# Expert passes of a mixture-of-experts step: token rows fetched by row number from device memory instead of by a product on TensorE

## The reference, cut to what matters

```python
logits = x.astype(f32) @ w_router.astype(f32) + b_router.astype(f32)
top_val, top_idx = lax.top_k(logits, TOP_K)
top_w = jax.nn.softmax(top_val, axis=-1)
gates = jnp.einsum('blk,blke->ble', top_w, jax.nn.one_hot(top_idx, N_EXPERTS, dtype=f32))
out = jnp.zeros(x.shape, f32)
for e in range(N_EXPERTS):
    out = out + gates[..., e:e + 1] * swiglu(x, wg[e], wu[e], wd[e]).astype(f32)
```

## Time and profile before

| what | value |
| --- | --- |
| median of 3 runs | 1713.34 us (1710.79 to 1714.33) |
| the profiled execution | 1714.72 us |
| its span in the trace | 1713.0 us |
| granted TensorE clock, mean over the span | 0.978 |
| PE busy | 1641.1 us (96%) |
| DVE busy | 1357.7 us (79%) |
| ACT busy | 1001.2 us (58%) |
| POOL busy | 59.1 us (3%) |

### The profile page before, as it was taken

The page is one execution under the profiler, slowest core; times in us unless marked ns, Lnnn a source line. Parts: engine busy times, 40 slices in busy tenths (PEclk is TensorE's granted clock), DMA queues, the critical chain, the costliest instruction groups (busy, mean ns, idle before and its releaser), DMA issues.

```text
span 1713.0 us, 25673 instructions
## 1 busy us (share of the span) xinstructions
PE 1641.1 (96%) x9611; PEld 1398.7 (82%) x9611; DVE 1357.7 (79%) x1480; ACT 1001.2 (58%) x923; POOL 59.1 (3%) x84
## 2 busy tenths in 40 slices
PE   7999999999999998999999999999999999999993
PEld 3878889998899797888888888888888888888883
DVE  5836656767676676988988988998988988989985
ACT  1222544443445236777777777777777777777771
POOL 2002000000000202000000000000000000000002
PEclk9999999999999999999999999999999999999997
DMA  6444245555354326999999999998998998998980
GB/s 160 128 135 123 91 143 165 180 160 173 108 158 155 82 74 220 321 376 336 348 376 326 354 373 329 347 376 329 353 371 314 371 368 313 375 372 309 370 331 25
DMA packets 209696, 441.84 MB, mean 258 GB/s; under 512 B 22896, under 2 KB 26912, under 8 KB 209614
## 3 DMA queue, kind: packets, MB, share of 16 engines
q1 hardware_dynamic: 205518, 435.18, 72.4%
q0 software_dynamic: 2048, 4.29, 1.4%
q10 hardware_dynamic: 2064, 1.45, 0.4%
HBM read 437.06 MB, written 1.93 MB: 256 GB/s over the span
## 4 chain that ended last, share of the span: by engine, by line
PE 80%; DVE 10%; issue 4%; ACT 2%; DMA 2%; SPq 1%; POOL 1%; DVEq 0%; ACTq 0%; POOLq 0%
PE bank L1642 77%; PE bank L1645 3%; DVE w_lo L991 2%; DVE piece_lo L991 2%; DVE ssm L991 2%; ACT piece_hi L735 1%; ACT y_hi L925 1%; DMA r_all<-in_b_glu_dram 1%; DMA piece<-in_w_proj_a_dram 1%; DVE r_all L991 0%; DVE wide L1405 0%; DVE ssm L1439 0%; DMA piece<-in_w_ffn_gate_dram 0%; DVE y_lo L1529 0%; DVE scr L991 0%
## 5 line engine op out<-in xcount | busy, mean ns | idle before, releaser
L991 DVE TENSOR_TENSOR w_lo<-weights,w_hi 128x2048 fp32r<-128x2048 f32 x336 | 765.1, 2289 | 98.6 <-ACT w_hi L934 94.7
L934 ACT ACTIVATE w_hi<-weights 128x2048 fp32r<-128x2048 f32 x336 | 644.4, 1920 | 191.3 <-PE bank L1642 191.2
L1642 PE MATMUL bank<-w_hi,xg_hi 128*128 128x512 f32 x896 | 357.4, 399 | 6.5 <-DVE xg_lo L991 5.0
L1642 PE MATMUL bank<-w_hi,xg_lo 128*128 128x512 f32 x896 | 350.6, 391 | 0.0
L1642 PE MATMUL bank<-w_lo,xg_hi 128*128 128x512 f32 x896 | 349.8, 390 | 0.0
L991 DVE TENSOR_TENSOR piece_lo<-piece,piece_hi 128x1024 fp32r<-128x1024 f32 x126 | 150.8, 1221 | 107.5 <-ACT piece_hi L735 104.3
L735 ACT ACTIVATE piece_hi<-piece 128x1024 fp32r<-128x1024 f32 x126 | 129.5, 1054 | 146.5 <-PE bank L1642 111.7
L1642 PEld LDWEIGHTS bank<-w_hi,xg_hi 128*128 128x128 f32 x896 | 168.6, 188 | 45.7 <-issue 6.9
L1642 PEld LDWEIGHTS bank<-w_hi,xg_lo 128*128 128x128 f32 x896 | 168.5, 188 | 36.9
L1642 PEld LDWEIGHTS bank<-w_lo,xg_hi 128*128 128x128 f32 x896 | 168.9, 189 | 32.9
L1642 PE MATMUL bank<-w_hi,hidT_hi 128*128 128x512 f32 x448 | 175.0, 391 | 0.0
(11 more groups left out here) (315 smaller groups left out, 2156.2 us busy)
## 6 DMA issues: line engine op xcount, KB each, us to landing
weights<-in_w_moe_gate_dram SPq DMA_DIRECT2D x112, 1024.0 KB, 7.3
weights<-in_w_moe_up_dram SPq DMA_DIRECT2D x112, 1024.0 KB, 7.3
weights<-in_w_moe_down_dram SPq DMA_DIRECT2D x112, 1024.0 KB, 6.8
piece<-in_w_in_dram SPq DMA_DIRECT2D x48, 512.0 KB, 3.8
piece<-in_w_ffn_gate_dram SPq DMA_DIRECT2D x22, 512.0 KB, 4.6
piece<-in_w_ffn_up_dram SPq DMA_DIRECT2D x22, 512.0 KB, 4.4
piece<-in_w_ffn_down_dram SPq DMA_DIRECT2D x22, 512.0 KB, 3.9
piece<-in_w_out_dram SPq DMA_DIRECT2D x16, 512.0 KB, 4.4
```

Source lines behind the costliest of these rows:

```text
L934: act.activation(w_hi[s % PAIRS][:, :], ring_slot[:, :], ACT.Copy).then_inc(w_hi_ready, 1)
L991: return dve.tensor_tensor(out, a, b, op)
L1642: signals(pe.matmul(out, lhsT, rhs, start=start, stop=stop, skip_group_check=True), signal)
```

## The change

The three tiles of token rows are no longer kept in SBUF in two parts. ACT copies them only into `acc`, and POOL writes them from there to device memory (`token_rows`, 264 rows of 1024, three DMAs). TensorE multiplies `pick` by a two-column tensor `token_no` that holds each token's number (three matmuls of two columns, `which_rows`), DVE converts the result to int32 (`which_i`), and POOL fetches the 128 rows that these numbers name into `xrow` by an indirect DMA (`gather`). In a pass this is done at chunk f = 4 (`NFC - 3`), for the next pass. The 12 matmuls of `rows_picked` and the two copies into `xrow` are gone, in the loop and ahead of it. The transposes of `xrow` stay where they were. POOL now runs the loop too. The loads of `ln2_g` and `ln2_b` stand behind POOL's loop.

```diff
+    if _f == NFC - 3:
+        PASS_TILES += [(("which",), "d", 6)]
+PASS_TILES += [(("hT", NFC - 1), "d", 6 + (NFC - 1) % 2)]
-PASS_TILES += [(("hT", NFC - 1), "d", 6 + (NFC - 1) % 2), (("picked", 0), "a", 2), (("picked", 1), "d", 3)]
...
+            for h, (at, m) in enumerate(TILES):
+                pool.wait_ge(emptied["a"], tiles.count["a"] - 6 + 2 * h + 2)
+                pool.dma_start(token_rows_dram[at:at + m, :], acc[0:m, h, :]).then_inc(rows_kept, 16)
+            pool.wait_ge(rows_kept, 16 * 3)
+            def gather():
+                pool.indirect_dma_start(out=xrow[:, :], out_offset=None, in_=token_rows_dram[:, :],
+                                        in_offset=bass.IndirectOffsetOnAxis(ap=which_i, axis=0)).then_inc(row_gathered, 16)
+            def turn():
+                pool.tensor_tensor(gather_turn, ones[:, 0:1], ones[:, 0:1], ALU.mult).then_inc(gather_turns, 1)
+            turn()
+            pool.wait_ge(which_ready, 1)
+            gather()
+            with all_passes(pool) as i:
+                wait_pass_emptied(pool, ("which",), i)
+                pool.wait_ge(xg_hi_ready, i * 2 + 2)
+                pool.wait_ge(gather_turns, i + 1)
+                turn()
+                gather()
...
-            act.wait_ge(router_zero, 1)
             for i in range(6):
-                p, h, at, ps = token_rows(i)
-                act.activation(xtok_hi[p, h, at], ps, ACT.Copy).then_inc(xtok_hi_ready, 1)
-                if i >= 3:
-                    act.activation(acc[p, h, at], ps, ACT.Copy).then_inc(emptied["a"], 1)
-            act.wait_ge(xtok_lo_ready, 3)
-            for i in range(3):
                 p, h, at, ps = token_rows(i)
                 act.activation(acc[p, h, at], ps, ACT.Copy).then_inc(emptied["a"], 1)
...
                 slots(pick, sel_of, 0, pick_ready)
+                dve.wait_ge(first_which, 1)
+                dve.tensor_copy(which_i, bank[0][:, 0:1]).then_inc(which_ready, 1)
...
+                        if f == NFC - 3:
+                            dve.wait_ge(row_gathered, i * 16 + 16)
+                            dve.tensor_copy(which_i, pass_tile_in(dve, ("which",), i)[:, 0:1]).then_inc(emptied["d"], 1)
                 hidden_lo(NFC - 1)
-                dve.tensor_copy(xrow[:, 512:D], pass_tile_in(dve, ("picked", 1), i)[:, :]).then_inc(emptied["d"], 1)
...
+            def which_rows(ps, signal):
+                for h in range(3):
+                    mm(ps[:, 0:2], pick[:, h, :], token_no[:, h, :], h == 0, h == 2, signal if h == 2 else None)
+            which_rows(bank[0], first_which)
             mm(bank[pass_bank[("ye", 0)]][:, :], spread[:, 0:P], y_hi[:, 0:512], True, True, filled)
+            fill(bank[pass_bank[("ye", 1)]], 12)
+            pe.wait_ge(row_gathered, 16)
...
+                        if f == NFC - 3:
+                            pe.wait_ge(pick_ready, i + 2)
+                            which_rows(claim_in_pass(("which",), i), filled)
                         down(f - 1)
                 hidden_transposed(NFC - 1)
-                pe.wait_ge(pick_ready, i + 2)
-                rows_picked(i)
                 down(NFC - 1)
```

More of the change, by code:

```diff
@@ L293, in trunk_kernel @@
             ssm = shared.enter_context(nc.sbuf_tensor("ssm", [P, SSM], F32))
-        xtok_hi = sb("xtok_hi", [P, 3, D], F32R)
-        xtok_lo = sb("xtok_lo", [P, 3, D], F32R)
         y_hi = sb("y_hi", [P, D], F32R)
@@ L299, in trunk_kernel @@
         spread = sb("spread", [P, 3 * P], F32R)
-        ROUTER = 2 * 3 * D + 2 * D + 2 * 3 * P
+        ROUTER = 2 * D + 2 * 3 * P
         sb("rest_of_ssm", [P, SSM - ROUTER])
@@ L440, in trunk_kernel @@
         ones = ssm[:, 19008:19008 + P]
-        assert 8960 == ROUTER
+        token_no = nc.alloc_sbuf_tensor_at("token_no", [P, 3, 2], F32R, offset=ssm_at + 4 * 19136)
+        token_i = ssm[:, 19144:19147].bitcast(I32)
+        which_i = ssm[:, 19152:19153].bitcast(I32)
+        gather_turn = ssm[:, 19160:19161]
+        token_rows_dram = nc.dram_tensor("token_rows", [T, D], F32, kind="Internal").ap()
         prm = r_all[0:96, 0:P]
@@ L483, in trunk_kernel @@
         xg_hi_ready, hidT_hi_ready = map(sem, ("xg_hi_ready", "hidT_hi_ready"))
-        first_picked, first_row_by_act, first_row_by_dve = map(
-            sem, ("first_rows_picked", "first_row_by_act", "first_row_by_dve"))
+        first_which, which_ready, rows_kept, row_gathered, gather_turns = map(
+            sem, ("first_rows_found", "rows_found", "token_rows_stored", "token_rows_gathered", "gather_turns"))
         router_zero, gslot_zero = map(sem, ("router_tiles_zero", "gslot_zero"))
-        xtok_hi_ready, xtok_lo_ready, xtok_lo_of_pool, y_hi_ready, spread_ready = map(
-            sem, ("xtok_hi_ready", "xtok_lo_ready", "xtok_lo_of_pool", "y_hi_ready", "spread_ready"))
+        y_hi_ready, spread_ready = map(sem, ("y_hi_ready", "spread_ready"))
         fvar_ready, fstd_ready, fscale_ready, y_out, y_out_step, y_stored = map(
@@ L693, in _ @@
             pool.memset(y_lo[:, :].bitcast(F32), 0.0).then_inc(router_zero, 1)
+            step(pool.iota(token_i, pattern=[[P, 3]], base=0, channel_multiplier=1))
+            pool.memset(token_no[:, :, :].bitcast(F32), 0.0).then_inc(router_zero, 1)
+            pool.wait_ge(router_zero, 7)
+            pool.tensor_copy(token_no[:, :, 0:1], token_i.unsqueeze(2)).then_inc(router_zero, 1)
             pool.wait_ge(router_zero, 8)
[L695 to L700, removed]
+            for h, (at, m) in enumerate(TILES):
[16 more added lines that the diff above has]
+                gather()
             for i, name in enumerate(("ln2_g", "ln2_b")):
@@ L963, in one_pass @@
                 hidden_hi(NFC - 1)
[L964 to L968, removed]
             act.wait_ge(npass_ready, 1)
@@ L1435, in slots @@
                 if ready is pick_ready:
-                    dve.wait_ge(router_zero, 3)
+                    dve.wait_ge(router_zero, 1)
                 for h, (_, m) in enumerate(TILES):
@@ L1481, in routing @@
                     dve.tensor_copy(sel_of[:, :, at], SEL)
[L1482 to L1487, removed]
                 ps = tile_in(dve, ("pos",))
@@ L1614, in _ @@
             routing()
-            dve.wait_ge(first_picked, 2)
-            dve.tensor_copy(xrow[:, 512:D], bank[1][:, :]).then_inc(first_row_by_dve, 1)
             dve.wait_ge(npass_ready, 1)
@@ L1952, in _ @@
             pe.wait_ge(sel_ready, 1)
-            pe.wait_ge(router_zero, 5)
+            pe.wait_ge(router_zero, 3)
             ps = claim(("pos",))
@@ L1966, in _ @@
             pe.wait_ge(router_zero, 8)
-            pe.wait_ge(xtok_lo_ready, 3)
-            pe.wait_ge(xtok_lo_of_pool, 3)
             pe.wait_ge(pick_ready, 1)
+            def which_rows(ps, signal):
+                for h in range(3):
+                    mm(ps[:, 0:2], pick[:, h, :], token_no[:, h, :], h == 0, h == 2, signal if h == 2 else None)
+            which_rows(bank[0], first_which)
             mm(bank[pass_bank[("ye", 0)]][:, :], spread[:, 0:P], y_hi[:, 0:512], True, True, filled)
+            fill(bank[pass_bank[("ye", 1)]], 12)
+            pe.wait_ge(row_gathered, 16)
             for n in range(2):
[L1972 to L1978, removed]
                 for kk in range(4):
@@ L2031, in hidden_transposed, with rows_transposed @@
                         turn_over(ps[:, P * n:P * n + P], hid_e[f % 2][:, P * n:P * n + P], P, filled if n == 3 else None)
-                def rows_picked(i):
+                def rows_transposed(i):
+                    pe.wait_ge(row_gathered, i * 16 + 32)
                     for n in range(2):
[L2035 to L2044, removed]
                         ps = claim_in_pass(("gather", n), i)
```

2 lines of the change are left out of this document (removed).

## The result

| | median us | lowest to highest, executions |
| --- | --- | --- |
| before | 1711.51 | 1706.53 to 1715.96, 20 |
| after | 1717.28 | 1713.59 to 1722.21, 20 |

The ratio is 1.0038, with a 95% interval of 1.0027 to 1.0048: the changed kernel is 6.5 us slower, 4.6 to 8.2. I had forecast 3.4 us less. The profiled execution of after took 1715.96 us, with a span of 1714.2 us and a mean granted clock of 0.974 (before: 0.978).

What follows compares the result with a forecast made beforehand. PE's stream was taken to bound the passes, with slack in DMA. Pass ends -4.6, small matmuls +2.4 and start -1.2 summed to -3.4 us, from 1713.34 to 1709.9 us; range 1706.5 to 1716.

Steps and rivals of the forecast that it cites:

- What leaves the passes: At each pass's end, removing the picks lets `down(6)` start 0.57 us earlier; eight times, -4.6 us.
- Rival 1: At the pass ends, the picks are worth their full time, 22.6 us, giving 1691.9 us; chance 3%.
- What enters the passes: At chunk 4, three two-column matmuls cost 0.30 us a pass, +2.4 us in all; DVE's one-column copy costs nothing.
- The gathers: Inside the passes, each gather is issued about 42 us ahead of its transposes and covered; adds 0.52 MB to 44.04 MB.
- Rival 3: In the passes, DMA is full and gathers push weight slots back, 1.3 us a pass, giving 1720.6 us; chance 8%.
- Ahead of the first pass: Before the loop, ACT freed of its `xrow` copy starts earlier: -1.2 us, if the first gather isn't late (4.4 us taken).
- rival 2: Ahead of the first pass, the first gather is slow; at 14.2 us, 1718.3 us; chance over 7 us 15%, over 12.6 us 2%.
- One sign that I had named for being wrong: Ahead of the loop, PE waiting for `xrow` would show the forecast wrong; no size given.
- Rival 4: At the loop's start, the first pass keeps its 2.4 GHz clock, 1.5 us less, giving 1708.4 us; chance 15%.
- The other 18 us of picks only covered a wait that is there anyway: At the pass ends, 18 of the picks' 22.6 us stand over the wait for `hidT_lo` and bring no gain.
- At each pass's end PE idles about 1.9 us behind the transposes: Expected sign at each pass's end: PE idles about 1.9 us before `down(6)`, released by DVE's `hidT_lo`.
- I had feared that `w_lo` would be stretched: In the loop, DVE's `w_lo` stretched beside POOL's gathers would show the forecast wrong; no size given.

Runs made afterwards that it cites:

- seven fills: After plus seven unread matmuls on `ident` between the last hidden rows' transposes and `down(6)`; 1708.14 us, ratio 0.9982 against before.
- three fills: After plus three unread matmuls on `ident` between the last hidden rows' transposes and `down(6)`; 1708.08 us, ratio 0.9982 against before.
- the kernel with the picks at chunk 4: Before, with its 12 picks and two `xrow` copies moved from the pass's end to chunk 4, no gather; 1736.68 us, ratio 1.0151 against before.
- the kernel with a start at full clock: After with `xrow` transposes before `down(6)`, last hidden transposes inside `down(5)`, `hidT` writes before the last slot, eleven unread matmuls ahead of the loop; 1691.37 us.
- the kernel with the early transposes: After, with the eight `xrow` transposes moved between the last hidden rows' transposes and `down(6)`; 1703.63 us, ratio 0.9954 against before.

## Why the prediction was wrong, point by point

**What leaves the passes: right.** I said that the picks covered a wait, and that `down(6)` could start only 0.53 to 0.77 us earlier. The distance from the transposes to `down(6)` fell from 3.18 us to 2.45, 0.73 us, of which 0.14 goes to the new burst: its first matmul is followed 0.10 us later than usual, the next ten 0.04 us in sum. That leaves 0.59 us, against 0.57. Rival 1, the full 22.6 us, is false.

**What enters the passes: right.** The three small matmuls, in PE's timeline of after at chunk 4 of the last pass:

```profile
1635.51 0.40 PE L1648 MATMUL bank<-w_hi,xg_lo 128*128 128x512 f32 x1
1635.74 0.39 PE L1648 MATMUL bank<-token_no,pick 128*128 128x2 f32 x3
1635.99 0.48 PE L1648 MATMUL bank<-w_hi,hidT_hi 128*128 128x512 f32 x1
1636.32 0.40 PE L1648 MATMUL bank<-w_lo,hidT_hi 128*128 128x512 f32 x1
```

They take 0.25 us and the matmul behind them 0.10 us more than usual: 0.35, against 0.30. Where the clock held, a pass was 125.25 us; my forecast came to 125.23.

**The gathers: right inside the passes.** POOL's timeline of after, ahead of the first pass and at chunk 4 of the second:

```profile
663.45 0.19 POOL L711 TENSOR_TENSOR ssm<-ssm 128x1 f32<-128x1 f32 x1 [3.95 <-DMA token_rows<-ssm]
664.32 1.05 POOL L707 DMA_INDIRECT xrow<-token_rows,ssm  x1 [0.68 <-DVE ssm L1502]
...
880.54 2.00 POOL L711 TENSOR_TENSOR ssm<-ssm 128x1 f32<-128x1 f32 x1 [123.71 <-DVE ssm L1589]
882.68 0.97 POOL L707 DMA_INDIRECT xrow<-token_rows,ssm  x1
```

And how long the nine gathers take to land, from the view of the tile `xrow`:

```profile
DMA to landing us min/median/max: 4.2/7.4/7.6
```

Weight slots land after 4.8, 7.2 and 14.3 us (lowest, median, highest), as before. The slowest are issued ahead of the passes; inside them the slowest takes 10.1 us, where before it was 8.5, and no engine waits for one. Rival 3, a full DMA, is false. What the forecast put at nothing is the 1.0 us in POOL's last `DRAIN`.

**Ahead of the first pass: near.** The first gather landed 4.2 us after its issue, where I took 4.4; rival 2 is false. PE in after:

```profile
663.16 0.67 PE L1648 MATMUL bank<-token_no,pick 128*128 128x2 f32 x3
...
664.01 2.84 PE L1648 MATMUL bank<-ident 128*128 128x128 f32 x24
668.56 1.09 PE L1651 MATMUL bank<-ident,xrow 128*128 128x128 f32 x8 [1.71 <-DMA xrow<-token_rows,ssm]
...
672.76 0.79 PE L1648 MATMUL bank<-w_hi,xg_hi 128*128 128x512 f32 x1 [2.88 <-DVE xg_lo L1001]
673.35 0.63 PE L1648 MATMUL bank<-w_lo,xg_hi 128*128 128x512 f32 x1
```

From the last transposes of the router (654.76 in after, 660.05 before) to the first product it takes 18.00 us instead of 18.86: -0.9 us, against -1.2. One pair of traces can't pin this term. In both, the sixteen matmuls on `ident` ahead of the small matmuls ran slow, 3.6 to 3.7 us in all; where they took 2.05 us, the same distance is 16.33 us with seven fills and 16.34 with three, whose code up to here is that of after, and 18.43 us in the kernel with the picks at chunk 4, whose code up to here is that of before: -2.1 us. The forecast lies between the two. The trunk up to the router's last transposes was 5.3 us shorter in this execution than in that of before; such scatter is why one profile against another misleads here (+1.2 us), and why parts are compared.

One sign that I had named for being wrong did show: PE waits 1.71 us for `xrow` ahead of the loop. It cost nothing. `xg_hi` is ready at 670.34, and `xg_lo`, which releases the first product, starts at 671.24, when DVE comes out of `w_lo`. Rival 4 is false: behind the first product nine matmuls last 0.62 to 0.63 us, the length at 1.2 GHz, where before it was seven of 0.61 to 0.63. So the first pass lost some 0.4 us more to the clock than before, by chance as far as the traces tell: twelve matmuls were slow with three fills, five in the kernel with the picks at chunk 4.

**The step that failed: "The other 18 us of picks only covered a wait that is there anyway", with "At each pass's end PE idles about 1.9 us behind the transposes".** The prediction saw this idle time, to a tenth, and used it in its sum as idle time alone. How fast PE runs behind it was a term that it put at nothing, without a reason. The granted clock had its place in the text, but only ahead of the first pass, where the profile of before already showed 0.52 behind idle PE; that row was the warning. In place of a free gap the runs showed a fall to 1.2 GHz behind most of the gaps, 1.58 us each. There was no rival for it, and the range ended at 1716.0. The sum, with the terms as the profiled execution has them: pass ends -4.7, small matmuls +2.8, start -0.9, falls 5 x 1.58 = +7.9, the slower start of the first pass +0.4, `DRAIN` +1.0, together +6.5 us.

The size fits across the executions. The kernel with seven fills is after without the falls; after is 1717.28 - 1708.14 = 9.1 us slower by the medians, which is 5.8 falls of 1.58 us. After's time goes with the mean granted clock of each execution: the five at 0.977 and 0.978 took 1713.59 to 1714.67 us, the nine at 0.973 to 0.975 took 1714.82 to 1721.29, and the six at 0.971 and 0.972 took 1719.71 to 1722.21. This alone would not show where the clock fell: in the kernel with a start at full clock, whose pass ends have no fall in the trace, the executions also go from 1687.88 us at 0.984 to 1695.27 us at 0.978.

What stays open: why the clock fell at five of the pass ends and held at three with the same 1.85 us ahead. The profile shows no difference in what the engines did before them.

## What to carry to other kernels

Work that looks redundant on the bound engine may stand over a wait. Before counting its removal as a gain, find what it covers, and price the hole twice: as idle time, and by what the granted clock does behind it; the profile shows both levels at the kernel's start already. If the clock falls, put useful work into the hole (here the transposes, 0.9 us a pass beyond the fill), and then move the producer so that there is no hole; after that the removal was worth some 20 us.

## What the runs showed of the hardware

**Short gaps count.** 1.85 us without matmuls was followed by 1.2 GHz at 5 of 8 pass ends in one kernel and at 6 of 8 in another; 1.18 us, 0.98 us and 0.29 us at none of eight each. A fall need not come at once: in the kernel with the early transposes the first product starts behind 2.26 us of idle PE, the next four matmuls follow at distances of 0.23 to 0.34 us, and only then the distances grow to 0.43 us.

**A one-column operation on POOL can take 2.0 us.** `turn` took 0.19 us ahead of the loop and 1.97 to 2.00 us in it, eight times. In the second pass it ran from 880.54 to 882.54; DVE at that place:

```profile
880.20 2.28 DVE L1001 TENSOR_TENSOR w_lo<-weights,w_hi 128x2048 fp32r<-128x2048 f32 x1
```

It begins 0.34 us ahead of POOL's operation, ends at 882.48, 0.06 us ahead of it, and is as long as always; the other seven times look the same. POOL waits for DVE, not the other way round. The Trainium skill (SBUF — State Buffer, Who interferes with whom) says that a DVE instruction with two inputs in SBUF contends with a GpSimd instruction that reads SBUF, and that the order of issue decides which of two waits; the trace agrees. I had feared that `w_lo` would be stretched.

**An indirect transfer of 128 rows of 4 KB** took 0.97 us of POOL in the loop, 1.05 us the first time. It landed after 4.2 us ahead of the passes and after 7.5 us (median of eight) beside the weight stream, about as late as a weight slot of twice the size (7.2 us).

**Transfers issued by POOL can be paid at the kernel's end.** POOL's last `DRAIN` took 4.07 us without a gather, 4.40 us with one and the three stores, and 5.05 us with nine; the other engines' last instructions stand behind it. What of POOL's new work makes it longer, transfers or `turn`, was not tried apart.
